# Six Strassen groups in place of four in each second feed-forward product, with the weight sums made in DRAM

## The reference

```
def conv_ffn(x, w_up, conv_w, conv_b, w_down):
    h = x @ w_up                                   # 2048 -> 2 * 5632
    h = sum(hp[:, j:j + T, :] * conv_w[j] for j in range(3)) + conv_b
    gate, val = jnp.split(h, 2, axis=-1)
    return (jax.nn.silu(gate) * val) @ w_down      # 5632 -> 2048
```

## Time and profile before

| | |
|---|---|
| Time, median of 3 runs | 3268.48 us (3267.51 to 3268.56) |
| The profiled execution: span from first to last instruction | 3266.7 us |
| The profiled execution: its time outside the span | not recorded; the median of the runs is 1.8 us above the span |
| TensorE busy, granted clock | 3249.2 us (99% of the span); full speed in nearly all slices |
| VectorE / ScalarE / POOL busy | 2387.4 (73%) / 1451.6 (44%) / 291.2 us (9%) |
| Weight loads (queue q1) | 592.35 MB, 50.3% of the 16 DMA engines' span |
| HBM read / written | 607.32 MB / 2.10 MB |

### The profile page before, as it was taken

One profiled execution on the slowest core, in us unless ns is written; L12 is line 12 of the kernel. 1 busy time (PEld: TensorE's weight loads), 2 busy tenths in 40 slices (PEclk: granted clock), 3 DMA queues, 4 the chain that ended last, 5 costly groups with the idle time before them and its releaser, 6 DMA issues.

```text
span 3266.7 us, 40565 instructions
## 1 busy us (share of the span) xinstructions
PE 3249.2 (99%) x17258; PEld 2803.1 (86%) x17258; DVE 2387.4 (73%) x2306; ACT 1451.6 (44%) x1140; POOL 291.2 (9%) x108
## 2 busy tenths in 40 slices
PE   9999999999999999999999999999999999999999
PEld 8888888888888888888888888888888898888887
DVE  7756778788889977768888889978866566554554
ACT  6534443333335455644333335465633334354433
POOL 1300001111120000000111110000012011000000
PEclk9999999999999999999999999999999999999999
DMA  7554445555555555455555555554555545545554
GB/s 274 186 201 179 168 168 194 185 189 193 187 188 204 202 207 182 141 193 186 189 193 189 186 192 193 208 207 178 181 194 200 193 160 182 184 158 189 206 182 154
DMA packets 89459, 616.23 MB, mean 189 GB/s; under 512 B 10432, under 2 KB 11584, under 8 KB 16704
## 3 DMA queue, kind: packets, MB, share of 16 engines
q1 hardware_dynamic: 84384, 592.35, 50.3%
q10 hardware_dynamic: 4896, 21.30, 1.9%
HBM read 607.32 MB, written 2.10 MB: 187 GB/s over the span
## 4 chain that ended last, share of the span: by engine, by line
PE 93%; DVE 4%; DVEq 1%; ACT 1%; issue 0%; DMA 0%; SPq 0%; ACTq 0%
PE acc L443 54%; PE acc L515 6%; PE acc L516 6%; PE acc L517 6%; PE acc L468 6%; PE acc L467 6%; PE acc L469 6%; DVE w_lo L326 1%; DVEq L1098 1%; PE acc L2209 0%; PE acc L1829 0%; PE acc L1893 0%; DVE over L1081 0%; PE acc L2313 0%; PE acc L551 0%; PE acc L2322 0%
## 5 line engine op out<-in xcount | busy, mean ns | idle before, releaser
L326 DVE TENSOR_TENSOR w_lo<-w_raw,w_hi 128x2048 fp32r<-128x2048 f32 x556 | 1350.8, 2433 | 618.9 <-ACT w_hi L322 615.3
L322 ACT ACTIVATE w_hi<-w_raw 128x2048 fp32r<-128x2048 f32 x556 | 1064.1, 1917 | 1443.0 <-PE acc L443 915.0
L443 PE MATMUL acc<-x_hi_lo,w_hi 128*128 128x512 f32 x5184 | 1213.7, 390 | 1.5 <-ACT w_hi L350 1.2
L443 PEld LDWEIGHTS acc<-x_hi_lo,w_hi 128*128 128x128 f32 x5184 | 960.8, 188 | 195.0 <-issue 3.5
L443 PEld LDWEIGHTS acc<-x_hi_lo,w_lo 128*128 128x128 f32 x5184 | 648.3, 191 | 17.1 <-DVE x_hi_lo L706 1.0
L443 PE MATMUL acc<-x_hi_lo,w_lo 128*128 128x256 f32 x5184 | 659.7, 284 | 1.2 <-DVE x_hi_lo L703 0.6
L467 PE MATMUL acc<-w_hi,x_hi_lo 128*128 128x512 f32 x736 | 288.2, 392 | 0.0
L469 PE MATMUL acc<-w_hi,x_hi_lo 128*128 128x512 f32 x736 | 286.5, 389 | 0.0
L468 PE MATMUL acc<-w_lo,x_hi_lo 128*128 128x512 f32 x736 | 286.4, 389 | 0.0
L515 PE MATMUL acc<-w_hi,hidden_hi_lo 128*128 128x512 f32 x672 | 262.5, 391 | 0.8 <-DVE w_lo L326 0.7
L517 PE MATMUL acc<-w_hi,hidden_hi_lo 128*128 128x512 f32 x672 | 261.5, 389 | 0.0
(11 more groups left out here) (295 smaller groups left out, 2587.8 us busy)
## 6 DMA issues: line engine op xcount, KB each, us to landing
w_raw<-weights_dram SPq DMA_DIRECT2D x556, 1024.0 KB, 4.8
over<-rows_dram ACTq DMA_DIRECT2D x9, 1024.0 KB, 7.5
w_raw<-weights_dram SPq DMA_DIRECT2D x7, 512.0 KB, 8.0
over<-over ACTq DMA_DIRECT2D x20, 128.0 KB, 2.5
resid<-x_tok_dram ACTq DMA_DIRECT2D x1, 2048.0 KB, 8.6
over<-w_gates_dram ACTq DMA_DIRECT2D x1, 2048.0 KB, 8.1
out_dram<-resid SPq DMA_DIRECT2D x8, 256.0 KB, 2.1
u_tiles<-x_dram SPq DMA_DIRECT2D x7, 256.0 KB, 7.4
```

The costliest lines, as they stand in the source:

```text
L322: act.activation(whi[:, n % NHI, :], w_raw(n), ACT.Copy).then_inc(weights_hi, 1)
L326: dve.tensor_tensor(w_lo(n, 0, CHUNK), w_raw(n), whi[:, n % NHI, :].bitcast(F32), ALU.subtract).then_inc(weights_split, 1)
L443: last = pe.matmul(acc[:, 4 * t + f, 0:cols], weights, moving(k, 0, cols), start=(k == 0 and low == low_first), stop=(k == CK * nch - 1 an ...
```

## The change

- `DOWN_PAIRS` becomes ((0, 1), (2, 3), (4, 5)): six groups a layer. A layer's down stage has 62 steps (20 chunk steps, 42 Strassen steps) in place of 56 (28 and 28). The leads are seven and three chunk steps.
- The sums are no longer made by VectorE. SP copies a block for each sum into a DRAM tensor `weight_sums` (24 copies of 1 MiB a layer, DRAM to DRAM). POOL then adds a second block (or an earlier sum) to each with an accumulating transfer in DRAM (24 a layer), three at a time after 8 of the 11 hidden products of the up stage. A sum is then loaded by SP as any other chunk, so every step has a load, a cast and a split.
- Layer 0's copies are issued behind the loads of chunks 12 to 69 (in `mix0_in` and `mix0_out`), layer 1's behind chunks `up0` + 8 to `up0` + 77, every third. The accumulating transfers of layer 0 lie in `up0`, those of layer 1 in `up1`.
- A third pair of features is mixed; its tiles lie at W0. VectorE's written order in the down stage is new. POOL's loop is unrolled.

```diff
-DOWN_GROUP = ("chunk", "b11", "t1", "chunk", "t3", "b22", "p2", "t4", "t2", "chunk")
-DOWN_PAIRS = ((0, 1), (2, 3))
-DOWN_LEAD = (8, 4)
+DOWN_GROUP = ("b11", "t1", "t3", "b22", "chunk", "p2", "t4", "t2")
+DOWN_PAIRS = ((0, 1), (2, 3), (4, 5))
+DOWN_LEAD = (7, 3)
...
+        SUM_FROM = {"t1": "b12", "t3": "b12", "t2": "b22", "t4": "p2"}
+        SUM_ADDS = {"t1": "b11", "t3": "b22", "t2": "t1", "t4": "t2"}
+        ADD_AFTER = {i: (kind, SUM_PLACES[a:b]) for i, kind, a, b in (
+            (0, "t1", 0, 3), (1, "t1", 3, 6), (2, "t3", 0, 3), (3, "t3", 3, 6), (5, "t2", 0, 3), (6, "t2", 3, 6),
+            (8, "t4", 0, 3), (9, "t4", 3, 6))}
...
+        def add_weights(pool, layer, i):
...
+            if i == 0:
+                pool.wait_ge(sum_begun, 16 * NSUM * (layer + 1))
+            if SUM_ADDS[kind] in SUM_KINDS:
+                pool.wait_ge(sum_made[SUM_ADDS[kind]], 16 * len(SUM_PLACES) * (layer + 1))
+            for p, j in places:
...
+                pool.dma_start(weight_sums[sum_index(layer, p, j, kind)], src, accum_op=ALU.add,
+                               max_dma_last_dim=4 * CHUNK).then_inc(sum_made[kind], 16)
...
+        def begin_sum(sp, layer, at):
...
+            sp.dma_start(weight_sums[sum_index(layer, *place, kind)], weight_block(layer, *place, SUM_FROM[kind]))\
+              .then_inc(sum_begun, 16)
+        for _layer, _first, _step in ((0, 12, 2.5), (1, CHUNK0["up0"] + 8, 3)):
+            for _i in range(NSUM):
+                BEGIN_AT[int(_first + _step * _i)] = (_layer, _i)
...
-            def group(p, j):
...
-                add(i0, t1, held_raw(held, "b11"), held_raw(held, "b12"))
...
+            def last_group(p):
+                i0 = down_at(p, NPAIR - 1, "b11")
+                splits(i0, i0 + 4)
+                take_p1(p)
+                split(i0 + 4)
+                o = take_r5_r7(p)
...
             splits(6, 8)
             mix(1)
+            split(8)
+            mix_lo(1)
+            splits(9, 12)
             dve.wait_ge(hid_ready, (layer + 1) * FG + 1)
-            group(0, 0)
-            group(0, 1)
+            mix(2)
+            split(12)
+            mix_lo(2)
+            splits(13, down_at(0, NPAIR - 1, "b11"))
+            i = last_group(0)
...
-            for r in range(NRAW, NRAWS):
-                sp.wait_ge(chunk_used, USED_BY[r - NRAW] + 1)
-                sp.dma_start(raw[:, r % NRAW, :], wd[r]).then_inc(raw_landed[r % NRAW], 16)
+            for n in range(NRAW, NCHUNKS):
+                sp.wait_ge(chunk_used, n - NRAW + 1)
...
+                if kind == "sum":
+                    summed, layer = SUM_KINDS[at0 % NSUM // len(SUM_PLACES)], at0 // NSUM
+                    sp.wait_ge(sum_made[summed], 16 * len(SUM_PLACES) * (layer + 1))
+                sp.dma_start(raw[:, n % NRAW, :], weight_sums[at0] if kind == "sum" else wd[at0])\
+                  .then_inc(raw_landed[n % NRAW], 16)
+                if n in BEGIN_AT:
+                    begin_sum(sp, *BEGIN_AT[n])
```

More of the change, by code:

```diff
@@ L66, in plain @@
                 c, n = chunks.pop(0)
-                steps.append({"kind": "chunk", "p": p, "c": c, "n": n, "raw": load(c, n)})
+                steps.append({"kind": "chunk", "p": p, "c": c, "n": n})
         plain(DOWN_LEAD[p])
-        for j, (c0, c1) in enumerate(DOWN_PAIRS):
-            held = {}
+        for j in range(NPAIR):
             for kind in DOWN_GROUP:
@@ L74, in down_steps, with down_block, sum_index, down_load @@
                     plain(1)
[L75 to L85, removed]
-                else:
-                    step["sum"] = {"t1": 0, "t2": 1, "t4": 0}[kind]
-                steps.append(step)
+                else:
+                    steps.append({"kind": kind, "p": p, "j": j})
         plain(len(chunks))
-    return steps, loads
-DOWN_STEPS, DOWN_LOADS = down_steps()
+    return steps
+DOWN_STEPS = down_steps()
 NDOWN = len(DOWN_STEPS)
-assert len(DOWN_LOADS) == 4 * (FT // CK)
+def down_block(p, j, kind):
+    row, side = {"b11": (0, 0), "b12": (0, 1), "p2": (1, 0), "b22": (1, 1)}[kind]
+    return 2 * p + side, DOWN_PAIRS[j][row]
+def sum_index(layer, p, j, kind):
+    return NSUM * layer + len(SUM_PLACES) * SUM_KINDS.index(kind) + SUM_PLACES.index((p, j))
+def down_load(layer, i):
+    e = DOWN_STEPS[i]
+    if e["kind"] in SUM_KINDS:
+        return "sum", sum_index(layer, e["p"], e["j"], e["kind"])
+    n, c = (e["n"], e["c"]) if e["kind"] == "chunk" else down_block(e["p"], e["j"], e["kind"])
+    return "weight", n * NK_DOWN + c
 def down_at(p, j, kind):
@@ L232, in program @@
         assert end <= W0 + WSIZE
[L233 to L237, removed]
+        mixed_at = (X0, X0 + 4 * MT * T, W0)
+        mixed = [place("mixed_hi_lo%d" % j, [P, 2, 4, 4, P], F32R, at0) for j, at0 in enumerate(mixed_at)]
+        mixed32 = [over(at0, [[P, 2, 4, 4, P]])[0][0] for at0 in mixed_at]
+        weight_sums = nc.dram_tensor("weight_sums_dram", (2 * NSUM, P, CHUNK), F32, kind="Internal").ap()
         stats = small[:, 0:48].rearrange("p (b q s) -> p b q s", b=2, q=4)
@@ L273, in program @@
         block_done = sem("block_done")
-        weights_sum = sem("weights_sum")
+        sum_begun = sem("sum_begun")
+        sum_made = {kind: sem("sum_made_" + kind) for kind in SUM_KINDS}
         mixed_raw = sem("mixed_raw")
@@ L935, in pool_hidden @@
             pool = nc.gpsimd
-            for i in loop(pool, FG):
+            for i in range(FG):
                 pool.wait_ge(gate_silu, layer * FG + i + 1)
@@ L984, in down_stationary @@
             if kind in MIXED:
-                return [mixed[:, j, part, MIXED[kind], kk, :] for part in range(2)]
+                return [mixed[j][:, part, MIXED[kind], kk, :] for part in range(2)]
             c, b = {"b11": (0, 0), "p2": (1, 0), "t4": (1, 1)}[kind]
             return features(DOWN_PAIRS[j][c], kk, b)
-        def sum_count(layer, e):
-            return 4 * (4 * layer + 2 * e["p"] + e["j"]) + SUM_AT[e["kind"]]
         def down_pe(pe, name):
@@ L1144, in take_r6 @@
             def take_r6(p):
-                used(down_at(p, 1, "t2"))
+                used(down_at(p, NPAIR - 1, "t2"))
                 return take(p, "t2", (((0, 1), PLUS), ((1, 0), MINUS), ((1, 1), PLUS)))
-            def group(p, j):
[L1149 to L1155, removed]
-                add(i0, t1, held_raw(held, "b11"), held_raw(held, "b12"))
[L1157 to L1176, removed]
             def splits(first, end):
```

128 lines of the change are left out of this document (62 added, 66 removed).

## The result

After the change the kernel takes 3278.3 us (median of 7 runs, 3276.63 to 3281.26) against 3268.48 us before (7 runs): a ratio of 1.003, 95% interval 1.002 to 1.004. It is slower by 9.8 us. The forecast was 3270.3 us, in a range of 3257 to 3292 us, with the largest chance (0.50) on "no change that can be told". The time lies in the stated range, but above the forecast's own range of 3263 to 3275 us.

A forecast was written before the change was run, and what follows sets the result against it. TensorE, busy 99% of the span, was taken as the bound. 3266.7 us + 0.8 (down stages) + 1.0 (transfers) = 3268.5 us of span, plus 1.8 from span to median: 3270.3 us, range 3257 to 3292.

The forecast's parts named there:

- Matmuls removed: Down stages: two more groups in two layers, 12 matmuls fewer per group, save 10.9 us; 223.0 us a stage without stalls.
- The lead of half 0: Start of each down stage: VectorE's mixings and splits make TensorE wait before steps 8, 9, 12, 13; 4.8 us a layer.
- The eviction in the last groups: Last group of each half: `take_p1` between two splits delays the chunk's split; 1.15 us lost, twice a layer.
- the step on loads in the groups: Down-stage groups: each short step's load has 0.6 us spare; cost 0, with 2 us a layer as upper end.
- The transfers: Copies and accumulating transfers beside the loads, `up0` fullest: 1 us over all stages, with 0 and 20 as ends.
- B: Rival: DMA engines fill in `up0`, from 9.6 us per copy plus accumulation; 20 us on the path, 3290 us; chance 0.24.
- A: Rival, down stages: VectorE keeps up and the lead's stalls don't come; total 3256 to 3261 us; chance 0.20.
- C: Rival, up stages: issuing an accumulation holds POOL over 12.1 us, so VectorE waits; 90 us at 14 us each; chance 0.05.
- The price of a copy: Copies between DRAM tensors: 1 MiB at 207 to 214 GB/s takes 4.9 us, an estimate near the 5.1 us upper end.

The follow-up runs named there:

- e6_all: The changed kernel with the edits of e1_early, e2_evict and e5_spread together: 3262.3 us, ratio 0.9982 to the kernel before.
- e1_early: The changed kernel with accumulating transfers after hidden products 0 to 7 without a gap, none under way when the up stage ends: 3272.5 us, ratio 1.0011.
- e5_spread: The changed kernel with the third mixing's six pieces spread between splits 13 and 20, and mix_lo and ScalarE's roundings moved later: 3273.9 us, ratio 1.0016.
- e3_no_traffic: The changed kernel without copies and accumulating transfers; each sum's load reads a plain weight block, so the output differs: 3271.2 us, ratio 1.0007.
- e7_before_copies: The kernel before the change with the 48 copies alone added, unused, and no accumulating transfer: 3268.5 us, ratio 1.0000.
- e4_before_traffic: The kernel before the change with the 48 copies and 48 accumulating transfers added at the same places, unused: 3275.2 us, ratio 1.0019.
- e2_evict: The changed kernel with evictions in each half's last group moved behind the chunk step's split and the next two splits: 3274.5 us, ratio 1.0017.

## Why the prediction was right or wrong

- **Matmuls removed: right.** 984 matmuls at 0.2267 us; 5.4 us a layer are there to be had, and e6_all has most of them.
- **The lead of half 0: right, by mechanism and size.** Forecast 0.5, 1.7, 1.0 and 1.6 us before steps 8, 9, 12 and 13; without the late load (e1_early) the distances give 0.3, 1.6, 0.7 and 1.5. e5_spread moved the third mixing and they went. VectorE was under 200 us (197) in the stage and was still what TensorE waited for: the share of a stage says little where the work stands in the wrong place.
- **The eviction in the last groups: right in three of four.** Forecast 1.15 us; 1.3, 1.2 and 1.2 measured, and 2.0 us in half 0 of `down0`. The rest there is the step on loads in the groups, taken at 0 with 2 us as its upper end: 0.7 us, since the cast of step 26 waited for its load: the loads there took 6.0 to 6.1 us to land in place of 4.8, and the 0.6 us that the prediction found spare were not enough (e1_early and e3_no_traffic).
- **Missed in the down stages: 0.7 us at the end of `down1`,** where the last split stands behind `finals` and the last steps are ordered by token block.
- **The transfers: the step that failed.** I wrote "I take 1 us over all stages" and took it from a stretch with a share of 0.77; e3_no_traffic shows 6.2 us. The sizes were inside the bounds: 2.6 us of the DMA engines for a copy, 3.9 us for an accumulation by the difference of shares and 5.2 us by the page's 7.6% for q0 (the two ways don't agree; why is open); `up0` came to 0.85, under one, and `up1`, at 0.74 and without copies, ended with the same late load. The share of a stage was the wrong quantity. Three accumulations issued at once fill the engines for some 24 us with the loads, whatever the mean is, and the load caught in it landed 2.6 us after its cast could have begun. I had granted each load 22 us of room before its matmuls. That room isn't there at the end of an up stage, where VectorE's written order has no idle time for the next 30 us. It cost 5.3 us of span as e1_early shows, with the clock's 1.6 us in it.
- **The range.** It was 35 us wide because B's price of 20 us was taken in. That the time fell into it doesn't speak for the transfer term, which was six times too small.
- **The rivals.** A needed the lead's stalls to stay away; they came. B had the engines full in `up0`. The place was near and the mechanism akin (a burst of three accumulations and the loads; the last copy had been issued at 863.5 us), and casts did wait for `w_raw` by DMA at the end of `up0`, but neither the sums nor the copies were late (SP issued the first load of a sum 21.95 us after the first matmul of `down0` in the change and in e1_early) and the price was 6 us, not 20. The burst is what decides, not the mean: under B's own point of 9.6 us for a copy and an accumulation together (2.6 + 3.9 = 6.5, or 7.8 with q0's 5.2) the loss was there. C didn't come: POOL issues three accumulations in 2.5 us.
- **The price of a copy.** From the Trainium skill (DMA: Bandwidth & Descriptors, "Latency and other measured facts") I took 4.9 us for a copy of 1 MiB, an estimate. The DMA engines were busy for 2.6 us with one (e7_before_copies), its time to landing was 7.1 us; the estimate lies between the two, and as a price in engine time it was too high. The Trainium skill's rule that transfers of all issuers interleave on the same 16 engines (same page, "Issuing engines are not separate DMA queues") agrees with the trace: the weight load in the burst waited although it has a queue of its own.
- **The time.** Forecast +1.8 us, measured +9.8. 0.8 us for the down stages became 2 x 231.4 - 460.0 = 2.8 us (mainly the 0.7 us at two places); 1 us for the transfers became 6.2 us. Together 9.0 of the 9.3 us of span.

## What to carry to other kernels

When work is taken off a busy engine, walk its written order through the stretch where the new steps stand, not its share of the stage: here 14 us less work a layer came with 7 us more stalls, and moving pieces of 0.7 to 2.5 us into the gaps behind the long steps brought them back. Transfers in the background are priced by their densest burst against the tightest moment of the loads beside them; the same 100 MB cost 6 us with a burst across a stage's end and 1 us without. What a matmul saving needs in extra loads, casts and splits decides whether it is kept.

## What the runs showed of the hardware

- An accumulating transfer of 1 MiB in DRAM took 3.9 us of the 16 DMA engines by the difference of shares in `up0` (e4_before_traffic less e7_before_copies), 1.5 times a copy's 2.6 us, and 5.2 us by its queue's share (q0: 7.6% of 3276 us for 48). POOL issued three in 2.5 us and was free again; they landed 16 us later.
- The granted clock can fall to its lower level after a short idle time of TensorE. After waits of 2.2 to 2.9 us it fell to about half for some 3 us in four cases (the change, e2_evict and e4_before_traffic in `down1`, e5_spread in `down0`) and in four others it stayed up (`down0` of the first three, `down1` of e5_spread). The length of the wait alone doesn't decide: it fell after 2.21 us (e5_spread) and stayed up after 2.30 (e4_before_traffic). It cost 1.5 to 1.8 us where it fell. After waits under 2 us (the longest was 1.8) it never fell in these stages. So a stall of 2.4 us can cost 4 (e4_before_traffic in `down1`).
- A single short wait widens the next matmul distance by about 0.1 us.
